# A 2-layer hybrid attention / PEER backbone on one core: weight ring from five blocks to four, u-row buffers from seven to eight

## Chip, cores and metric

One Trainium2 chip, one core. The metric is the device time of one execution in microseconds (us), lower is better.

## The reference, cut to what is computed

Two token streams of 256 tokens, width 1024 (latent `x`, context `ctx`), pass two layers. Each layer has a token mixer (attention, in layer 0 with retention) and a PEER channel mixer; each is fed by an RMS norm with gains and shifts that come from a conditioning vector. All in float32.

```python
for l in range(2):
    # six modulation vectors from silu(c) @ mod_w[l]  (1024 x 6144)
    hx = modulate(x_lat, norm1_g[l], sh1, sc1)            # ctx likewise
    yx, yc = mixer(hx, hc, w_in, w_out, ...)               # projections, attention/retention, output projection
    x_lat = x_lat + g1 * yx
    x_lat = x_lat + g2 * peer(modulate(x_lat, norm2_g[l], sh2, sc2), w_q, sub_keys, u, v)
    # the context stream does the same in layer 0 only

def peer(h, w_q, sub_keys, u, v):                          # per token: 8 heads x 16 experts = 128 rows
    q = h @ w_q                                            # 1024 x 2048
    # scores against 2 x 128 sub-keys per head, top 16 of each, top 16 of their 256 sums -> idx
    act = gelu(einsum('td,ted->te', h, u[idx]))
    return einsum('te,ted->td', softmax(top_s) * act, v[idx])
```

`u` and `v` have 16384 rows of 1024 floats (4 KB) each. Six token tiles of 128 tokens go through PEER (four in layer 0, two in layer 1), so 6 x 128 = 768 gathers of 128 rows are made from `u` and 768 from `v`.

## The kernel before

The engines' programs are written out by hand; they meet at semaphores, and each engine runs strictly in its own order.

**Weights.** All weights (blocks of `mod_w`, the input and output projections, the query projection `w_q`) stream through one ring `W` of `NW` = 5 blocks of 512 KB. The SP queue issues 240 loads in order (L497); load n waits until the block in its place, n − NW, is freed (L490, quoted below). Blocks come in groups of four, (half, part) = (0,0), (0,1), (1,0), (1,1). A group serves a piece of a product 512 columns wide: each token tile that uses it (a "unit") runs 4 matmuls of half 0 and then 4 of half 1, each of them two instructions in the profile, so 16 instructions a unit and 4 instructions a block. The first two blocks of a group are freed together when the last unit has finished half 0 (`pr_half`, `op_half`), the last two when it has finished half 1 (`pr_mm`, `op_mm`); for `mod_w` two blocks are freed after each half (`mod_mm`), for `w_q` after each pair of query heads (`pq_mm`). With five blocks, the first block of the next group is loaded while the present group is in use; the other three follow as blocks are freed.

```python
if n >= NW:
    sp.wait_ge(*blocks[n - NW][7])
```

**Gathers.** GpSimd (POOL) issues all row gathers (`u_gather`, `v_gather`, issued at L512): one gather brings 128 rows of 4 KB, 512 KB. A "slot" is one of a tile's 128 experts per token. POOL's order is two u gathers, then two v gathers which lie LAG = 36 slots behind; the first 36 slots of a window are u gathers alone. A u gather waits until the dot product `NU` = 7 slots back is done (`u_dot`, VectorE L2032), a v gather until the matmul that used its buffer is done (`v_used`, TensorE L1084). Since POOL runs in order, a u gather that waits also holds the v gathers behind it. There are two windows, tiles 0 to 3 and tiles 4 and 5. When a window's u gathers are over, its last 36 v gathers use the u buffers too.

**Beside the gathers.** The dense work of later tiles (projections, attention, retention, query scores, top-16) is cut into steps that all engines run between slots, at slots given by the table `BESIDE`. TensorE, VectorE and ScalarE take these steps in the same order as their part of the gathers.

**Before the first window** run, in this order on TensorE: four column blocks of layer 0's modulation (`ada`, L580), norm1, the projection of the context tiles (`proj(0)`, L692: 12 units in six groups of two), attention and retention of the context beside eight more blocks of `mod_w`, and the output projection (`outp(0)`, L939: four units in two groups). Meanwhile POOL loads 32 blocks of layer 1's `mod_w` into free u and v buffers (u buffers 4, 5, 6 and v buffers 5, 6) at the pace at which VectorE sums them (L1485, L1488).

**Start.** A table of biases, gains and conditioning vectors is loaded into ring block 4 (`sm`, L478 to L483) and turned by two transposes (`setup_t`); load 4 waits for them (L488). `H2` holds the normed rows of PEER and is not in use until much later.

## Time and profile before

| | us |
|---|---|
| time, 3 runs | 2670.25 median (2651.04 to 2674.83) |
| the profiled execution | 2671.68 |
| its span in the profile | 2669.9 |
| busy: TensorE (PE) | 1717.8 (64%) |
| busy: VectorE (DVE) | 1738.0 (65%) |
| busy: GpSimd (POOL), issuing gathers | 1477.8 (55%) |
| busy: ScalarE (ACT) | 377.7 (14%) |
| moved by DMA | 959.07 MB, mean 359 GB/s |

### The profile page before, as it was taken

What the parts mean: (1) busy time and instruction counts of PE and PEld (TensorE: products, weight loads), DVE (VectorE), ACT (ScalarE), POOL (GpSimd) and SP (SyncE); (2) the same over time, 40 slices, a digit from 0 to 9 for tenths busy, and PEclk for the clock granted to TensorE, in tenths of its full rate; (3) what the DMA queues carried; (4) which work ended last, traced back from release to release, by engine and by line L of the source; (5) the groups of instructions that cost most, each with busy time, mean ns of one, the idle gap of its engine ahead of it and who ended that gap; (6) DMA issues with size and microseconds to landing.
All of it is one profiled execution on the core that took longest, in us unless ns stands there. A gap on an engine that the chain in (4) does not pass through costs nothing.

```text
span 2669.9 us, 23151 instructions
## 1 busy us (share of the span) xinstructions
PE 1717.8 (64%) x7250; PEld 784.4 (29%) x7250; DVE 1738.0 (65%) x4297; ACT 377.7 (14%) x790; POOL 1477.8 (55%) x1575
## 2 busy tenths in 40 slices
PE   6899966776987764555434655677637975444335
PEld 2446652222445331222101111234432442211000
DVE  2733598776789776676645766644696776667641
ACT  1021112111122110010001211111112210101000
POOL 1100136666666766666666675771256566767774
PEclk8968987888566876666555776568867576766556
DMA  7774599999999999999999999993699899999998
GB/s 254 268 244 158 173 322 357 406 406 404 406 372 362 405 400 406 405 406 407 408 406 405 376 393 407 409 409 151 236 347 398 320 366 400 407 405 409 409 409 337
DMA packets 312521, 959.07 MB, mean 359 GB/s; under 512 B 30144, under 2 KB 65104, under 8 KB 312016
## 3 DMA queue, kind: packets, MB, share of 16 engines
q0 software_dynamic: 225792, 822.18, 78.9%
q1 hardware_dynamic: 82448, 127.47, 13.6%
q10 hardware_dynamic: 4160, 7.95, 0.8%
q8 instruction: 59, 0.97, 0.1%
q14 instruction: 62, 0.51, 0.1%
HBM read 956.43 MB, written 1.05 MB: 359 GB/s over the span
## 4 chain that ended last, share of the span: by engine, by line
DMA 37%; PE 23%; DVE 19%; POOL 11%; issue 8%; ACT 1%; SPq 0%; POOLq 0%; ACTq 0%; DVEq 0%
DMA u_rows<-in_peer_u,idx 21%; DMA v_rows<-in_peer_v,idx_turned 10%; DVE u_rows L2032 9%; POOL v_rows L512 6%; POOL u_rows L512 5%; PE ps L1084 4%; PE ps L692 4%; PE ps L732 2%; PE ps L569 2%; PE ps L750 2%; PE ps L939 2%; PE ps L580 1%; DMA wring<-in_ab_w_in 1%; DMA u_rows<-in_peer_v,idx_turned 1%; PE ps L1049 1%
## 5 line engine op out<-in xcount | busy, mean ns | idle before, releaser
L2032 DVE CUSTOM_DVE_ANT_0 u_rows<-ps,u_rows 128x1024 f32<-128x1024 f32 x768 | 926.6, 1221 | 441.2 <-DMA u_rows<-in_peer_u,idx 407.3
L512 POOL DMA_INDIRECT u_rows<-in_peer_u,idx x768 | 724.3, 943 | 668.1 <-DVE act_w L2032 370.5
L1084 PE MATMUL ps<-v_rows,spread_w 128*32 128x512 f32 x2736 | 543.1, 878 | 627.7 <-DMA v_rows<-in_peer_v,idx_turned 616.2
L512 POOL DMA_INDIRECT v_rows<-in_peer_v,idx_turned x684 | 648.6, 948 | 228.1 <-issue 188.5
L1084 PEld LDWEIGHTS ps<-v_rows,spread_w 128*32 128x32 f32 x2736 | 71.8, 127 | 931.0 <-issue 910.1
L692 PE MATMUL ps<-wring,arena 128*128 128x512 f32 x528 | 279.3, 679 | 27.2 <-DVE arena L1519 9.1
L692 PEld LDWEIGHTS ps<-wring,arena 128*128 128x128 f32 x528 | 109.0, 217 | 201.3 <-issue 155.6
L1049 PE MATMUL ps<-arena,wring 128*128 128x128 f32 (+1 forms) x768 | 159.1, 374 | 5.8 <-DMA wring<-in_peer_w_q 3.8
L1049 PEld LDWEIGHTS ps<-arena,wring 128*128 128x128 f32 x768 | 138.5, 243 | 60.7 <-issue 42.7
L569 PE MATMUL ps<-table,arena 128*128 128x128 f32 x432 | 97.3, 364 | 77.4 <-ACT arena L1137 31.0
L550 POOL DMA_DIRECT2D u_rows<-in_mod_w x20 | 14.7, 735 | 213.9 <-DVE v_rows L1488 161.0
L569 PEld LDWEIGHTS ps<-table,arena 128*128 128x128 f32 x432 | 63.0, 180 | 175.7 <-issue 74.4
L732 PE MATMUL ps<-arena 64*128 64x512 f32 (+2 forms) x128 | 101.6, 892 | 4.1 <-DVE mod_cols L1499 2.8
L939 PE MATMUL ps<-wring,arena 128*128 128x512 f32 x160 | 78.4, 640 | 9.6 <-ACT arena L1295 6.5
L750 PE MATMUL ps<-arena 128*128 128x64 f32 x416 | 83.0, 364 | 2.5 <-DVE arena L1676 2.3
L750 PEld LDWEIGHTS ps<-arena 128*128 128x128 f32 x416 | 82.8, 290 | 3.6 <-DVE arena L1676 2.7
L1392 ACT ACTIVATE act_w<-act_w 128x16 f32<-128x16 f32 x48 | 10.3, 216 | 513.1 <-DVE act_w L2032 512.9
L1362 ACT ACTIVATE arena<-ps 128x128 f32<-128x128 f32 (+1 forms) x48 | 14.8, 311 | 464.4 <-PE ps L1049 464.4
L1084 PE MATMUL ps<-resid,spread_w 128*32 128x512 f32 x192 | 41.3, 914 | 46.6 <-DMA resid<-in_peer_v,idx_turned 45.2
L580 PE MATMUL ps<-wring,silu_c 128*32 128x512 f32 x256 | 60.2, 930 | 7.9 <-DMA wring<-in_mod_w 7.8
L2032 DVE DVE_READ_ACCUMULATOR2_ANT act_w<- 128x1 f32 x768 | 63.7, 83 | 0.0
L1392 ACT ACT_TABLE_LOAD x47 | 60.3, 1283 | 0.8
(254 smaller groups left out, 1983.5 us busy)
## 6 DMA issues: line engine op xcount, KB each, us to landing
wring<-in_mod_w SPq DMA_DIRECT2D x64, 512.0 KB, 5.0
wring<-in_peer_w_q SPq DMA_DIRECT2D x64, 512.0 KB, 10.4
wring<-in_ab_w_in SPq DMA_DIRECT2D x56, 512.0 KB, 8.1
u_rows<-in_peer_u,idx POOLq DMA_INDIRECT x768, 13.6
wring<-in_swa_w_in SPq DMA_DIRECT2D x24, 512.0 KB, 10.7
v_rows<-in_peer_v,idx_turned POOLq DMA_INDIRECT x684, 13.4
u_rows<-in_mod_w POOLq DMA_DIRECT2D x20, 512.0 KB, 6.5
wring<-in_ab_w_out SPq DMA_DIRECT2D x16, 512.0 KB, 7.1
```

The lines of the kernel that those rows point to most:

```text
L512: nc.gpsimd.indirect_dma_start(out=rows, out_offset=None, in_=table, in_offset=bass.IndirectOffsetOnAxis(ap=index, axis=0)).then_inc(lande ...
L569: return nc.tensor.transpose(dst, src, ident[0:n, 0:n])
L580: mm = nc.tensor.matmul(MP(l, b)[32 * q:32 * q + 32, :], SC[:, 4 * half + q, :], w[:, q % 2, :], start=half == 0, stop=half == 1, skip_gro ...
L692: mm = nc.tensor.matmul(PS[:, unit_bank(u), :], HT[:, 4 * half + k, (t % 2) * P:(t % 2 + 1) * P], w[:, k % 2, :], start=half + k == 0, sto ...
L732: nc.tensor.matmul(PS[:, i % 2, 0:nk], q, k, start=True, stop=True).then_inc(at_s, 1)
L750: mm = nc.tensor.matmul(value_out(n, m), PT[:, m % 2, c, :], val, start=c == 0, stop=c == len(kts) - 1)
L939: mm = nc.tensor.matmul(PS[:, u % 2, :], HT[:, 4 * half + k, (t % 2) * P:(t % 2 + 1) * P], w[:, k % 2, :], start=half + k == 0, stop=half ...
L1049: mm = nc.tensor.matmul(PS[:, hp % 2, 0:nt * P], w[:, k % 4, (hp % 2) * P:(hp % 2 + 1) * P], HT[:, k, lo:lo + nt * P], start=k == 0, stop= ...
L1084: mm = nc.tensor.matmul(PS[32 * q:32 * q + 32, 6 + e, :], spread_w[:, s // PAIR % 2, 32 * c:32 * c + 32], v_buffer(v_place(x)[0])[:, e * 5 ...
L1362: nc.scalar.activation(QTB[:, hp % 2, 0:nt * P], PS[:, hp % 2, 0:nt * P], ACT.Copy).then_inc(pq_ev, 1)
L1392: nc.scalar.activation(av_[:, 1, g % 2, :], av_[:, 0, g % 2, :], ACT.Gelu).then_inc(act_done, 1)
L2032: nc.vector.tensor_tensor_reduce(UB[:, slot % NU, :], HP, UB[:, slot % NU, :], 1.0, 0.0, ALU.mult, ALU.add, av_[:, 0, g % 2, j:j + 1]).the ...
```

## The change

`NW` goes from 5 to 4 and `NU` from 7 to 8; the two arrays together keep their size (a block and a u buffer are both 4 KB per partition). The start table moves from ring block 4 to `H2[:, 1, :]`, and the wait of load 4 for the transposes goes, since load 4 now waits for block 0 to be freed. Semaphore arrays and the tables of v buffers follow from `NW` and `NU`.

```diff
-NW = 5
+NW = 4
-NU = 7
+NU = 8
...
-            sm = W[:, 4, :]
+            sm = H2[:, 1, :]
...
             for n, (_, kind, l, b, split, half, part, _) in enumerate(blocks):
-                if n == 4:
-                    sp.wait_ge(setup_t, 2)
                 if n >= NW:
                     sp.wait_ge(*blocks[n - NW][7])
...
-            turn(PS[:, 6, 0:P], W[:, 4, 0:P]).then_inc(setup_t, 1)
-            turn(PS[:, 7, 0:16], W[0:16, 4, P:2 * P], 16).then_inc(setup_t, 1)
+            turn(PS[:, 6, 0:P], H2[:, 1, 0:P]).then_inc(setup_t, 1)
+            turn(PS[:, 7, 0:16], H2[0:16, 1, P:2 * P], 16).then_inc(setup_t, 1)
```

On the SP queue the loads keep their order and what changes is what each waits for. At the start of the program, with the semaphore that each load waits for (`mod_mm`: a half of a modulation block is done; `pr_half`, `pr_mm`: a unit's first or second half is done), before:

```order
L483 DMA wring<-in_c_ctx 8x128
L497 DMA wring<-in_mod_w 128x2x512 x4
L497 DMA wring<-in_mod_w 128x2x512 [waits setup_t]
L497 DMA wring<-in_mod_w 128x2x512 [waits mod_mm] x11
L497 DMA wring<-in_ab_w_in 128x2x512 [waits mod_mm] x5
L497 DMA wring<-in_ab_w_in 128x2x512 [waits pr_half] x2
```

and with the change:

```order
L483 DMA h<-in_c_ctx 8x128
L495 DMA wring<-in_mod_w 128x2x512 x4
L495 DMA wring<-in_mod_w 128x2x512 [waits mod_mm] x12
L495 DMA wring<-in_ab_w_in 128x2x512 [waits mod_mm] x4
L495 DMA wring<-in_ab_w_in 128x2x512 [waits pr_half] x2
L495 DMA wring<-in_ab_w_in 128x2x512 [waits pr_mm] x2
```

Five projection loads stood ahead of the first wait for a unit, now four do: the first block of the second group has moved behind `pr_half`.

On POOL's queue the u and v gathers of both windows keep their order; at the end of the first window the last 36 v gathers take the buffers in another turn. There stands before:

```order
L512 DMA v_rows<-in_peer_v,idx_turned 128x1024 x2
L512 DMA u_rows<-in_peer_v,idx_turned 128x1024 x7
L512 DMA v_rows<-in_peer_v,idx_turned 128x1024 x8
L512 DMA u_rows<-in_peer_v,idx_turned 128x1024 x7
L512 DMA v_rows<-in_peer_v,idx_turned 128x1024 x8
L512 DMA u_rows<-in_peer_v,idx_turned 128x1024 x6
L512 DMA u_rows<-in_peer_u,idx 128x1024 x38
```

and with the change:

```order
L510 DMA v_rows<-in_peer_v,idx_turned 128x1024 x2
L510 DMA u_rows<-in_peer_v,idx_turned 128x1024 x8
L510 DMA v_rows<-in_peer_v,idx_turned 128x1024 x8
L510 DMA u_rows<-in_peer_v,idx_turned 128x1024 x8
L510 DMA v_rows<-in_peer_v,idx_turned 128x1024 x8
L510 DMA u_rows<-in_peer_v,idx_turned 128x1024 x4
L510 DMA u_rows<-in_peer_u,idx 128x1024 x38
```

Sixteen buffers turn there in place of fifteen; the next window starts with 38 u gathers in both.

## Rows read from the trace of the kernel before

**Rows 1.** The page: busy tenths and GB/s in 40 equal slices.

```profile
PE   6899966776987764555434655677637975444335
...
DMA  7774599999999999999999999993699899999998
GB/s 254 268 244 158 173 322 357 406 406 404 406 372 362 405 400 406 405 406 407 408 406 405 376 393 407 409 409 151 236 347 398 320 366 400 407 405 409 409 409 337
```

**Rows 2.** Windows by stage: busy of each engine, granted clock, DMA share, GB/s.

```profile
82.00:98.00 16.00, 15.33 (x49) 7.45 (x48) 14.34 (x26) 1.99 (x5) 3.90 (x6) 1.00 0.79 268
98.00:117.00 19.00, 15.94 (x46) 7.18 (x45) 14.10 (x25) 0.60 (x1) 3.75 (x6) 1.00 0.77 272
...
450.00:1800.00 1350.00, 857.50 (x3473) 346.17 (x3473) 943.00 (x2304) 198.60 (x389) 893.61 (x944) 0.68 1.02 400
```

**Rows 3.** Chain of work that ended last, projection of the context: start us, us, what.

```profile
85.48 6.19 DMA wring<-in_ab_w_in
...
91.72 1.98 PE ps L692 x4
93.70 0.44 PE ps L569 x4
94.14 0.79 PE ps L597 x8
94.92 6.99 PE ps L692 x16
...
101.93 9.11 DMA wring<-in_ab_w_in
```

**Rows 4.** Timeline of PE, 95 to 118 us.

```profile
105.68 1.98 PE L692 MATMUL ps<-wring,arena 128*128 128x512 f32 x4 [1.63 <-DMA wring<-in_ab_w_in]
108.55 1.98 PE L692 MATMUL ps<-wring,arena 128*128 128x512 f32 x4 [0.88 <-DMA wring<-in_ab_w_in]
111.09 1.98 PE L692 MATMUL ps<-wring,arena 128*128 128x512 f32 x4 [0.56 <-DMA wring<-in_ab_w_in]
```

**Rows 5.** Waits of PE, 0 to 50 us: total us, times, longest.

```profile
PE ps L580 <- DMA wring<-in_mod_w: 7.8, 5, 3.3
```

**Rows 6.** Timeline of PE, 204 to 240 us.

```profile
219.11 1.94 PE L580 MATMUL ps<-wring,silu_c 128*32 128x512 f32 x8
...
223.52 1.07 PE L580 MATMUL ps<-wring,silu_c 128*32 128x512 f32 x8
...
225.90 1.06 PE L580 MATMUL ps<-wring,silu_c 128*32 128x512 f32 x8
```

**Rows 7.** DMA issues by line, 160 to 318 us: count, KB, median us to landing.

```profile
wring<-in_mod_w SPq DMA_DIRECT2D x27, 512.0 KB, 4.7
wring<-in_ab_w_out SPq DMA_DIRECT2D x8, 512.0 KB, 4.7
```

**Rows 8.** Waits of the whole program: total us, times, longest.

```profile
POOL u_rows L512 <- DVE act_w L2032: 379.2, 282, 9.2
...
POOL v_rows L512 <- PE ps L1084: 36.0, 54, 3.3
```

**Rows 9.** Windows where the DMA engines pause beside gathers, columns as in rows 2.

```profile
318.00:400.00 82.00, 60.85 (x271) 50.40 (x269) 69.18 (x214) 12.53 (x36) 34.57 (x37) 0.87 0.92 320
400.00:440.00 40.00, 18.54 (x67) 7.78 (x68) 32.16 (x89) 9.03 (x16) 25.45 (x27) 0.63 0.92 325
...
780.00:850.00 70.00, 63.90 (x288) 40.42 (x288) 67.39 (x132) 21.45 (x35) 43.27 (x46) 0.65 0.92 336
...
1520.00:1550.00 30.00, 14.79 (x62) 4.45 (x61) 24.19 (x58) 8.88 (x13) 16.20 (x17) 0.73 0.83 307
...
1920.00:2000.00 80.00, 31.72 (x166) 26.06 (x165) 77.38 (x225) 9.84 (x25) 39.03 (x42) 0.68 0.92 327
...
2080.00:2160.00 80.00, 75.33 (x278) 40.15 (x278) 60.21 (x152) 20.40 (x50) 44.71 (x48) 0.56 0.88 311
```

**Rows 10.** DMA issues by line, 450 to 650 us, columns as in rows 7.

```profile
wring<-in_ab_w_in SPq DMA_DIRECT2D x19, 512.0 KB, 11.0
...
u_rows<-in_peer_u,idx POOLq DMA_INDIRECT x68, 18.2
```

**Rows 11.** Timeline of PE in the second window, 2008 to 2220 us.

```profile
2010.67 6.70 PE L692 MATMUL ps<-wring,arena 128*128 128x512 f32 x8 [1.72 <-DVE g_row L1452]
...
2018.29 3.70 PE L692 MATMUL ps<-wring,arena 128*128 128x512 f32 x8
...
2033.12 3.11 PE L692 MATMUL ps<-wring,arena 128*128 128x512 f32 x4 [1.89 <-DMA wring<-in_swa_w_in]
...
2215.21 2.08 PE L1049 MATMUL ps<-arena,wring 128*128 128x128 f32 x8 [3.79 <-DMA wring<-in_peer_w_q]
```

## The prediction

> **What bounds the kernel now.** I read the page's 40 slices first [rows 1]. They show three regimes. From the seventh slice (400 us) to the 27th (1800 us), and from about 2000 us on, the DMA engines are busy nine tenths or more and move 400 to 409 GB/s: the gathers. In the first five slices TensorE is busy eight or nine tenths and DMA moves 158 to 268 GB/s: the dense work before the first gather, fed by the weight ring. Around slice 28 (1800 to 1900 us) there are no gathers at all. The windows by stage say the same with numbers: from 450 to 1800 us the DMA share is 1.02 with TensorE at 857 of 1350 us, while from 82 to 117 us TensorE works 31 of 35 us at full clock and DMA is at 0.77 to 0.79 [rows 2]. So a larger u buffer can gain only where DMA pauses beside gathers, and a smaller ring can lose mainly where there are no gathers: there TensorE's delay is the program's delay, and it moves everything behind it.
>
> **Ring from five to four, projection of the context.** The chain of waits shows this stage alternating between L692 and a load of `ab_w_in` [rows 3]. A load is issued at 85.48, when a unit's second half ends; it lands 6.19 us later, at 91.67; the four instructions that use this block start at 91.72; then come two short pieces and a whole unit (6.99 us for 16 instructions, so 1.75 us for a block's four), and the next load of the chain is issued at 101.93. With five blocks the first of a group is already there, so the load at 85.48 is the group's fourth block, the third of the four issued after the last unit's first half. With four blocks it becomes the group's third, and the fourth is issued directly behind it. It must be used after the third, so each change of group costs at least its 1.75 us where the loads come close together, and the distance between landings where they come slower. TensorE waits before each of three blocks in a row at 105.68, 108.55 and 111.09, so landings there are (111.09 - 105.68) / 2 = 2.7 us apart [rows 4]. Six groups have five changes: 4 x 1.75 + 2.7 = 9.7 us. Lower bound 0, if something else on the way is later (the rows name nothing); upper bound five times the widest distance, 108.55 - 105.68 = 2.87, so 14.4.
>
> **Modulation at the start.** TensorE waits 7.8 us in five pieces for `mod_w` here [rows 5]. The fifth load, which started as soon as the small table was turned, must now wait for block 0, and from then on two pairs of loads take turns. I count the pair's second block (1.3 us at 400 GB/s for 512 KB) once behind the longer wait and about 1.2 us over the following three groups: 2.5 us. Bounds: 0, if the engines' rate sets this stage anyway, and 7.8, if the waits double. The wait on the transposes that goes is worth nothing, since a later one takes its place.
>
> **Modulation beside attention, output projection.** With four blocks, the pair for a half is issued when the half before the previous one ends. Near the end of this stage one half runs 219.11 to 221.05 and the half after next starts at 225.90 [rows 6], which leaves 4.85 us; loads land in a median of 4.7 us here [rows 7], and the pair's second a little later: 0.5 us. Where halves are farther apart it costs nothing. In the output projection the first block of the second group used to be there; now it is issued half a unit (3.5 us) ahead of its use and takes 4.7 [rows 7]: 1 us. Bounds for both together 0 to 3. Before the gathers the ring costs 9.7 + 2.5 + 0.5 + 1.0 = 13.7 us, between 0 and 25.
>
> **The ring beside gathers.** Here loads land later (11.0 us [rows 10]) and TensorE already waits for the last block of a group, 1.89 us before 2033.12 and 3.79 us before 2215.21 [rows 11]. These waits will grow by some 2 to 6 us at perhaps four places. Queued behind them on TensorE are matmuls of v rows, which hold v buffers, and VectorE steps that hold dot products. But the DMA engines stay at 1.02 [rows 2] with up to fifteen gathers issued ahead, 15 x 1.3 = 19 us of work, so nearly all of it is covered: 2 us, between 0 and 10.
>
> What the row says of a deeper gather queue: a weight block issued into it lands after 11.0 us, a u gather after 18.2 [rows 10], so blocks pass the gathers that wait. The Trainium skill (DMA: Bandwidth & Descriptors, "Queues, rings and completion order") has the rule for it: each DMA engine takes turns between the queues that have work, a packet at a time. By that rule the eighth gather adds nothing to a block's time; if instead blocks stood in one line with the gathers, each would land one gather (1.3 us) later and the 2 us above would be about 5. The trace agrees with the rule.
>
> **u buffers from seven to eight.** POOL waits 379.2 us in 282 pieces for a dot product before a u gather, and only 36.0 us for v buffers [rows 8]. Most of this costs nothing, as DMA is full meanwhile. What can be won is the time in which DMA pauses, 1.03 less the share, times the length [rows 9]: 82 x 0.11 = 9.0; 40 x 0.11 = 4.4; 70 x 0.11 = 7.7; 30 x 0.20 = 6.0; 80 x 0.11 = 8.8; 80 x 0.15 = 12.0; 47.9 us in all. One more buffer lets POOL run one slot farther ahead before it stops: a u gather and the v gather behind it, 2 x 1.3 = 2.6 us of DMA work for each stall, or 1.3 us where only u gathers are issued. It does not make VectorE or TensorE faster, so a stretch in which one of them is always busy gains once, not at every pause. VectorE works 69 of 82, 67 of 70 and 77 of 80 us in the first, third and fifth window, TensorE 75 of 80 in the last [rows 9]. So I take each window as one stall: 1.3 for the first and the fifth, which begin with u gathers alone, 2.6 for the other four: 13.0 us. Bounds: 0, and all 47.9. I stay near the low end, because four of six windows are bound by an engine.
>
> **Moved v gathers.** In a window's last 36 v gathers one more buffer turns. DMA runs at 409 GB/s there [rows 1], so nothing is won or lost.
>
> **Sum.** 13.7 + 2.0 - 13.0 = +2.7 us. On the profiled execution's 2671.7 us that is 2674.4. This execution lies 1.4 us above the median of the three runs, 2670.25, so I forecast 2673. About 1% is what a measurement of this kernel can tell from no change: its three runs span 0.9%.
>
> **Rivals.**
>
> *Pauses are short and separate (faster).* POOL's waits for dots average 379.2 / 282 = 1.3 us [rows 8], less than the 2.6 us of an added slot. If the DMA pauses in the six windows are made of such pieces with recoveries between, four fifths of 47.9 go: -38 + 13.7 + 2 = -22, and 2648 us. Against it: VectorE or TensorE hardly rest in four of the windows. Chance 0.14.
>
> *Depth buys nothing.* If every pause is the engine's own pace, and the extra gather is repaid in the next stretch, only the losses stay: +15.7, 2686 us. For it speaks the same busy time; against it, the window from 1520 to 1550 with one long wait (9.2 us at most [rows 8]). Chance 0.16.
>
> *TensorE's clock falls in the early stage (slower by over 1%).* The clock is granted at full there with waits up to 1.63 us between blocks [rows 2, 4]. With four blocks each group waits longer, at its first block too. If that brings the lower level, 1.2 GHz, matmuls take about twice as long: eight instructions of L692 took 6.70 us in one place and 3.70 in the next [rows 11]. A group has 32 instructions of 0.44 us: 14 us more for each group that runs slowly. With one group the time is 2687, with two 2701; it decides from the second group on. The Trainium skill (TensorE: Matmul & The Clock Gate, "Part 1: The HAM clock gate") says that the throttled clock is the default and activity releases it, which speaks for this rival; the full clock in rows 2 in spite of waits speaks against it so far. Chance 0.12.
>
> The forecast, losses and gains about equal, has 0.58. Its own range is 2660 to 2687. The range of 8 in 10 takes in the first two rivals and one slow group: 2648 to 2700. Faster by over 1% (under 2643.5) needs most of the first rival: 0.11. Slower by over 1% (over 2697) comes from the clock, or from losses at their upper bounds with no gain: 0.13. Within 1%: 0.76.
>
> **What would show it.** In the trace of the changed kernel the first u gather should be issued about 14 us later than before. TensorE should wait for `ab_w_in` between 50 and 150 us some 10 us more in total, now before a group's first and fourth block too, at an unchanged clock. The six windows of rows 9, shifted by the same 14 us, should together lose about 35 us instead of 48. Elsewhere the DMA share should stay at 1.02 to 1.03. The prediction is wrong in its first part if the first gather is not late, in its second if the pauses shrink by over 25 us or not at all, and in its cover if DMA shows new pauses at changes of weight group beside gathers.

## The result, and the profile after

| | before | with the change |
|---|---|---|
| time, median of 20 runs (us) | 2655.16 (2642.04 to 2674.83) | 2675.78 (2664.42 to 2699.03) |
| ratio, runs set against each other | | 1.0062, 95% [1.0039, 1.0085] |
| the profiled execution (us) | 2671.68 | 2682.0 |
| its span (us) | 2669.9 | 2680.2 |

The change makes the kernel 0.62% slower, 16.5 us at 2655: little, but the interval leaves out 1. The medians of the table are 20.6 us apart; the ratio, made from runs set against each other, is the figure used below, and its interval, 10.4 to 22.6 us, holds both. All ratios leave out executions more than 1.5% above the fastest of their kernel, which touches e3 (four of twelve) and e12 (two of twelve) below most. The forecast of 2673 us lies 3 us from the new median, and that closeness flatters it. The profiled execution before, from which the sum was made, was near the slow end of the 20 runs, which spread over 33 us: it lies 16.5 us above their median. The working gave +2.7 us, and +16.5 were measured. So what has to be explained is a difference of 14 us in a sum that "came out right".

The page of the changed kernel, its busy tenths and its rates, and the DMA issues, answering to [rows 1]:

```profile
PE   6899975766887765555444655677647974445335
...
DMA  6766499999999999999999999993799899999998
GB/s 226 253 230 204 135 332 348 405 406 405 405 387 347 406 400 406 406 404 408 408 406 406 401 372 407 409 409 146 244 359 405 317 358 366 407 404 409 409 409 349
```

The three regimes stand as before. In the first two slices DMA moves less than in [rows 1] (226 and 253 GB/s for 254 and 268): with a block less in flight the weights come more slowly. From slice 8 most slices read 400 to 409 again.

Waits of PE in the changed kernel, 0 to 50 us and 50 to 165 us (total us, times, longest); before they were [rows 5] and, for `ab_w_in`, 7.5 us in 8 pieces:

```profile
PE ps L578 <- DMA wring<-in_mod_w: 12.0, 6, 4.6
...
PE ps L690 <- DMA wring<-in_ab_w_in: 14.8, 11, 4.2
```

The timeline of PE in the projection of the context (the idle time ahead of each piece in brackets), answering to [rows 4]:

```profile
101.92 7.11 PE L690 MATMUL ps<-wring,arena 128*128 128x512 f32 x16
108.87 0.60 PE L567 MATMUL ps<-table,arena 128*128 128x128 f32 x4
111.81 5.37 PE L690 MATMUL ps<-wring,arena 128*128 128x512 f32 x8 [2.34 <-DMA wring<-in_ab_w_in]
118.89 1.98 PE L690 MATMUL ps<-wring,arena 128*128 128x512 f32 x4 [1.71 <-DMA wring<-in_ab_w_in]
121.29 1.13 PE L690 MATMUL ps<-wring,arena 128*128 128x512 f32 x2 [0.42 <-DMA wring<-in_ab_w_in]
```

A unit of 16 instructions runs without a pause, and then comes the wait that did not exist before, ahead of the first block of the next group (2.34), and further ones ahead of its third and fourth. That is the edit read directly. The eight instructions at 111.81 also took 5.37 us where eight took 3.70 at 97.13: the granted clock was 0.72 from 112 to 118 us.

Two single instructions give milestones. The end of the projection is the end of its last matmul, the start of the gathers is the first u gather on POOL. In the changed kernel, from the timelines of PE and of POOL:

```profile
164.80 1.88 PE L690 MATMUL ps<-wring,arena 128*128 128x512 f32 x4
...
325.56 1.01 POOL L510 DMA_INDIRECT u_rows<-in_peer_u,idx  x1 [47.09 <-DVE idx L1956]
```

and in the kernel before:

```profile
151.31 1.88 PE L692 MATMUL ps<-wring,arena 128*128 128x512 f32 x4
...
317.75 1.01 POOL L512 DMA_INDIRECT u_rows<-in_peer_u,idx  x1 [46.17 <-DVE idx L1958]
```

The projection ends 13.5 us later, but the first gather is only 7.8 us later. Between them lies attention beside eight blocks of modulation, and there TensorE's granted clock differed. Windows of before and of after, 164 to 237 us, columns as in [rows 2]. Before:

```profile
164.00:237.00 73.00, 72.43 (x313) 39.85 (x314) 20.88 (x65) 13.91 (x37) 0.00 (x0) 0.61 0.65 220
```

After:

```profile
164.00:237.00 73.00, 69.94 (x333) 35.08 (x331) 23.09 (x69) 15.09 (x42) 1.45 (x2) 0.77 0.79 261
```

TensorE is busy nearly all the time in both, and its clock reads 0.61 before and 0.77 after. More instructions are done in less busy time. Whether this belongs to the change is a question for repeats (below: it does not).

Beside the gathers, three views. First the waits of POOL over the whole program, answering to [rows 8]:

```profile
POOL u_rows L510 <- DVE act_w L2030: 272.1, 242, 10.3
...
POOL v_rows L510 <- PE ps L1082: 161.3, 133, 7.0
```

The wait for a dot product has gone from 379.2 to 272.1 us, as the edit promises, and the wait for a v buffer from 36.0 to 161.3. The queue stops in another place, not less. Second, the six windows of [rows 9], moved by the delay of their gathers:

```profile
326.00:408.00 82.00, 60.13 (x270) 50.12 (x269) 69.37 (x216) 12.75 (x36) 35.92 (x39) 0.88 0.93 328
408.00:448.00 40.00, 18.79 (x69) 7.96 (x70) 32.60 (x90) 9.02 (x16) 24.85 (x26) 0.65 0.87 312
...
788.00:858.00 70.00, 58.20 (x287) 36.83 (x285) 67.35 (x134) 21.45 (x35) 41.02 (x43) 0.71 0.90 335
1528.00:1558.00 30.00, 14.01 (x62) 4.36 (x60) 25.05 (x62) 8.88 (x13) 18.00 (x20) 0.73 0.94 351
1927.00:2007.00 80.00, 32.87 (x173) 26.39 (x172) 77.39 (x225) 9.83 (x25) 40.60 (x44) 0.68 0.94 341
2087.00:2167.00 80.00, 75.39 (x279) 40.30 (x278) 59.85 (x151) 20.41 (x50) 43.75 (x48) 0.56 0.87 304
```

By the prediction's own measure, 1.03 less the share, they lose 8.2 + 6.4 + 9.1 + 2.7 + 7.2 + 12.8 = 46.4 us; before they lost 47.9. Only the fourth window is plainly better (0.83 to 0.94, 3.3 us), and the 100 us after it are worse, 1.01 at 395 GB/s, where before they had 1.03 at 406.

Third, a place where a pause is new: the last group of `w_q` blocks. Timeline of PE in the changed kernel, with [rows 11] at 2215.21 as its counterpart:

```profile
2218.98 1.06 PE L1082 MATMUL ps<-v_rows,spread_w 128*32 128x512 f32 x8
2224.21 1.39 PE L1047 MATMUL ps<-arena,wring 128*128 128x128 f32 x8 [4.17 <-DMA wring<-in_peer_w_q]
2230.23 2.08 PE L1047 MATMUL ps<-arena,wring 128*128 128x128 f32 x8 [4.63 <-DMA wring<-in_peer_w_q]
```

the instruction of VectorE and the gather of POOL that are released behind it:

```profile
2232.77 0.30 DVE L1869 MAX8 top_vals<-ps 128x8 f32<-128x128 f32 x1 [9.88 <-PE ps L1035]
...
2236.49 0.94 POOL L510 DMA_INDIRECT u_rows<-in_peer_u,idx  x1 [9.92 <-DVE act_w L2030]
```

and the window around it:

```profile
2222.00:2242.00 20.00, 9.54 (x58) 4.65 (x58) 9.91 (x28) 1.56 (x2) 7.09 (x8) 0.74 0.83 301
```

Before, one wait of 3.79 us stood here, POOL's longest wait was 5.74 us, and DMA did not pause:

```profile
2212.00:2232.00 20.00, 9.34 (x46) 3.62 (x50) 15.02 (x41) 1.56 (x2) 11.05 (x12) 0.65 1.04 394
```

The order of events fits one chain: TensorE waits twice for weights, so VectorE's top-16 has no scores, so its next dot product is late, so POOL does not issue, and after some ten us the queue of gathers runs dry: 20 x (1.04 - 0.83) = 4.2 us of DMA lost.

### The profile page after: what moved, and what is told of

Same layout as the page of the kernel before. It is cut to its first block, busy times and chain, and to the rows that moved or that the text cites. A ratio compares the mean times of both kernels' runs of the same rounds, so it can differ in the third digit from the quotient of the medians.

```text
span 2680.2 us, 23151 instructions
## 1 busy us (share of the span) xinstructions
PE 1691.3 (63%) x7250; PEld 777.4 (29%) x7250; DVE 1734.3 (65%) x4297; ACT 377.9 (14%) x790; POOL 1476.1 (55%) x1575
## 4 chain that ended last, share of the span: by engine, by line
DMA 40%; PE 24%; DVE 17%; POOL 9%; issue 7%; ACT 1%; SPq 0%; ACTq 0%; POOLq 0%; DVEq 0%
DMA v_rows<-in_peer_v,idx_turned 20%; DMA u_rows<-in_peer_u,idx 13%; DVE u_rows L2030 7%; POOL v_rows L510 5%; PE ps L1082 5%; PE ps L690 5%; POOL u_rows L510 4%; PE ps L937 2%; DMA wring<-in_ab_w_in 2%; PE ps L1047 2%; PE ps L730 2%; PE ps L567 2%; DMA u_rows<-in_peer_v,idx_turned 2%; PE ps L578 1%; PE ps L748 1%
## 5 line engine op out<-in xcount | busy, mean ns | idle before, releaser
L2030 DVE CUSTOM_DVE_ANT_0 u_rows<-ps,u_rows 128x1024 f32<-128x1024 f32 x768 | 926.9, 1221 | 441.2 <-DMA u_rows<-in_peer_u,idx 406.1
L1082 PE MATMUL ps<-v_rows,spread_w 128*32 128x512 f32 x2736 | 526.5, 858 | 630.3 <-DMA v_rows<-in_peer_v,idx_turned 620.0
L690 PE MATMUL ps<-wring,arena 128*128 128x512 f32 x528 | 273.2, 666 | 38.2 <-DMA wring<-in_ab_w_in 16.5
L1047 PE MATMUL ps<-arena,wring 128*128 128x128 f32 (+1 forms) x768 | 168.9, 390 | 10.9 <-DMA wring<-in_peer_w_q 8.8
L1047 PEld LDWEIGHTS ps<-arena,wring 128*128 128x128 f32 x768 | 146.0, 254 | 67.0 <-issue 47.0
L730 PE MATMUL ps<-arena 64*128 64x512 f32 (+2 forms) x128 | 94.4, 831 | 4.1 <-DVE mod_cols L1497 2.8
L937 PE MATMUL ps<-wring,arena 128*128 128x512 f32 x160 | 77.7, 631 | 16.1 <-ACT arena L1293 6.5
L1360 ACT ACTIVATE arena<-ps 128x128 f32<-128x128 f32 (+1 forms) x48 | 14.8, 311 | 468.2 <-PE ps L1047 468.2
L578 PE MATMUL ps<-wring,silu_c 128*32 128x512 f32 x256 | 61.3, 823 | 12.3 <-DMA wring<-in_mod_w 12.3
L1869 DVE MAX8 top_vals<-ps 128x8 f32<-128x128 f32 x80 | 22.1, 293 | 68.6 <-PE ps L1035 66.7
L2030 DVE DVE_READ_ACCUMULATOR2_ANT act_w<- 128x1 f32 x768 | 63.7, 83 | 0.0
## 6 DMA issues: line engine op xcount, KB each, us to landing
wring<-in_peer_w_q SPq DMA_DIRECT2D x64, 512.0 KB, 10.5
```

The costliest lines, as they stand in the source:

```text
L578: mm = nc.tensor.matmul(MP(l, b)[32 * q:32 * q + 32, :], SC[:, 4 * half + q, :], w[:, q % 2, :], start=half == 0, stop=half == 1, skip_gro ...
L690: mm = nc.tensor.matmul(PS[:, unit_bank(u), :], HT[:, 4 * half + k, (t % 2) * P:(t % 2 + 1) * P], w[:, k % 2, :], start=half + k == 0, sto ...
L730: nc.tensor.matmul(PS[:, i % 2, 0:nk], q, k, start=True, stop=True).then_inc(at_s, 1)
L937: mm = nc.tensor.matmul(PS[:, u % 2, :], HT[:, 4 * half + k, (t % 2) * P:(t % 2 + 1) * P], w[:, k % 2, :], start=half + k == 0, stop=half ...
L1047: mm = nc.tensor.matmul(PS[:, hp % 2, 0:nt * P], w[:, k % 4, (hp % 2) * P:(hp % 2 + 1) * P], HT[:, k, lo:lo + nt * P], start=k == 0, stop= ...
L1082: mm = nc.tensor.matmul(PS[32 * q:32 * q + 32, 6 + e, :], spread_w[:, s // PAIR % 2, 32 * c:32 * c + 32], v_buffer(v_place(x)[0])[:, e * 5 ...
```

## Experiments

All time is cut at five instructions, the starts of the first u gather and of the dot products (L2032, after the change L2030) number 1, 512, 513 and 768, and at the projection's two ends (the end of its first instruction and of its last). "Window 1" is from the first to the 512th dot product, "window 2" from the 513th to the 768th. The kernels of a job share runs of the kernel before; the first column of times is those shared runs' median.

| kernel | job, before | ratio, 95% | projection from, to | clock 164 to 237 | first u gather | window 1 | window 2 |
|---|---|---|---|---|---|---|---|
| before, profiled first | 2655.2 | | 50.7, 153.2 | 0.61 | 317.8 | 1444.6 | 702.0 |
| with the change | 2655.2 | 1.0062 [1.0039, 1.0085] | 54.3, 166.7 | 0.77 | 325.6 | 1444.2 | 706.3 |
| e1 before | A 2783.75 | 1.0022 [0.9983, 1.0061] | 50.9, 151.5 | 0.75 | 308.3 | 1507.9 | 746.9 |
| e2 ring 4, u 7 | A | 1.0088 [1.0058, 1.0119] | 52.2, 162.9 | 0.56 | 329.2 | 1500.7 | 754.6 |
| e3 the change | A | 0.9998 [0.9956, 1.0041] | 51.5, 162.3 | 0.93 | 309.3 | 1488.1 | 750.1 |
| e4 change + 1 early place | A | 0.9957 [0.992, 0.9995] | 50.4, 153.1 | 0.62 | 316.3 | 1478.1 | 757.6 |
| e5 ring 4, u 7 | B 2812.72 | 1.0056 [1.0022, 1.0089] | 51.4, 162.5 | 0.63 | 328.2 | 1521.7 | 761.9 |
| e6 ring 5, u 6 | B | 1.0061 [1.0024, 1.0099] | 50.9, 151.7 | 0.55 | 322.7 | 1535.5 | 762.2 |
| e7 ring 5, u 7, 9 early places | B | 0.9913 [0.9875, 0.9951] | 48.1, 140.1 | 0.83 | 295.7 | 1501.0 | 757.1 |
| e8 ring 4, u 8, 9 early places | B | 0.9886 [0.9832, 0.9941] | 48.2, 139.2 | 0.97 | 284.1 | 1505.8 | 763.1 |
| e9 ring 4, u 7, v 9 | C 2662.51 | 1.0088 [1.0048, 1.0128] | 53.5, 167.7 | 0.55 | 339.7 | 1443.9 | 709.5 |
| e10 ring 4, u 7 | C | 1.0080 [1.0042, 1.0117] | 52.8, 164.4 | 0.88 | 315.9 | 1443.7 | 710.0 |
| e11 change + 1 early place | C | 1.0021 [0.9988, 1.0054] | 50.8, 152.8 | 0.75 | 307.4 | 1444.7 | 703.0 |
| e12 ring 4, u 8, 9 early places | C | 0.9949 [0.9912, 0.9987] | 48.5, 139.0 | 0.61 | 309.9 | 1445.8 | 705.8 |

Jobs A, B and C ran on three different chips. In A and B the same kernel takes 2784 and 2813 us, 5 to 6% more than in the first comparison and in job C. The expectations put this down to the chip; but each chip was measured in one job only, so it can't be told apart from whatever else differed then. The difference turned out to be useful: it separates the two halves of the change. e8 has six timed executions, e9 seven, the other kernels of the jobs twelve.

**Job A: is it the ring, is it the depth?**

e1 is the kernel before, unchanged, as a measure of what a ratio of equal kernels looks like.

> The kernel before, a second time, as a yardstick: a ratio of 1.000 within its interval, and a second profile of the same program. Theory A (the two profiles of before and after differ partly by TensorE's granted clock between 150 and 240 us, which is not a part of the change): the first u gather is issued up to 8 us earlier or at the same time as in the first profile (317.8 us), and the clock between 164 and 237 us differs from 0.61. Rival B (the clock there follows from the program): clock and first gather as in the first profile, within 1 us.

It measured 1.0022 [0.9983, 1.0061]. With the clock at 0.75 where the first trace of the same program had 0.61, its first gather came at 308.3 instead of 317.8: the same program, so the rival, that the clock follows from the program, is out.

e2 undoes one half of the change:

```diff
 NW = 4
-NU = 8
+NU = 7
```

> Ring of four alone, seven u buffers as before. Theory A (the early stage pays for the ring, the eighth u buffer bought next to nothing): 14 to 18 us slower than before, ratio about 1.006, the same as the changed kernel within 3 us; context projection done 13 to 14 us late as in the changed kernel. Rival B (the eighth buffer returns the 13 us that I forecast and the ring costs more than forecast, beside the gathers too): 27 to 30 us slower than before, ratio about 1.011.

It measured 1.0088, between the two forecasts (1.006 and 1.011): the ring of four costs 25 us by itself on this chip.

e3 is the changed kernel again.

> The changed kernel beside the others on the same chip: ratio 1.004 to 1.009 as measured. Theory A: within 3 us of the run with four blocks and seven u buffers. Rival B: 10 us or more faster than that run.

It measured 0.9998 [0.9956, 1.0041], below the range expected, and the rival's case came true. Here the change is no loss that the interval shows. Against e2, run beside it, the eighth buffer gives 0.9%, 25 us; by the plain means of all twelve executions each (1.0019 and 1.0087 of before's) it is 0.7%, 19 us. In the two traces window 1 is 12.6 us shorter and window 2 4.5 us; the 19.9 us between their first gathers go with the clock (0.93 and 0.56).

e4 keeps the change, but until the gathers begin the eighth u buffer serves as a fifth place of the ring. Loads below a limit may take extra places; POOL waits for the last use of such a place before its first gather.

```diff
+        EXTRA = [(UB[:, 7, :], 84)]
+        w_in = [sem(f"w_in{i}") for i in range(NW + len(EXTRA))]
...
+        for n in range(len(blocks)):
+            freed, k = free_w.pop(0)
+            while k >= NW and n >= EXTRA[k - NW][1]:
+                freed, k = free_w.pop(0)
...
+            for k in range(NW, NW + len(EXTRA)):
+                if EXTRA[k - NW][1] == 84:
+                    pool.wait_ge(*W_LAST[k])
```

> The changed kernel, but u buffer 7, which is idle until the gathers, serves as fifth place of the ring for the first 84 loads (up to the output projection). Theory A (the loss is made before the first gather): the whole 14 to 16 us come back, ratio to before 0.998 to 1.001; PE waits for mod_w and ab_w_in before 165 us are 15 us in total as before, not 27. Rival B (the ring of four also costs beside the gathers, out(3) and the last query projection above all): only 8 to 10 us come back and the ratio stays at 1.002 to 1.004.

It measured 0.9957, below the range expected. The projection ends at 153.1 like before's, so the early loss is the ring's fifth place and nothing else of the change. Against e3 the place gives 0.4%, 11 us, near the 11 us between before's and the ring of four's projections in this job (151.5, and 162.9 and 162.3).

**Job B: each size against its neighbours.**

e5 repeats e2.

> Ring of four and seven u buffers once more, since the chip of the last four runs was about 5% slower than the one of the changed kernel's first timing, and the changed kernel's ratio differed between them (1.006 there, 1.000 here). Theory A (the ring costs the same on any chip, 0.6 to 0.9%; the eighth buffer is worth nothing where DMA runs at 405 GB/s without pause and about 0.9% where it pauses): ratio to before 1.006 to 1.009 in either case. Rival B (the ring's cost itself depends on the chip): ratio under 1.003 or over 1.012.

1.0056, just under the range expected: the loss repeats, a little smaller.

e6 goes the other way in depth, with the ring as it was (one early `mod_w` block moves from u buffer 6 to v buffer 7):

```diff
-NU = 7
+NU = 6
...
-        EARLY_W = [UB[:, 4, :], UB[:, 5, :], UB[:, 6, :], VB[:, 5, :], VB[:, 6, :]]
+        EARLY_W = [UB[:, 4, :], UB[:, 5, :], VB[:, 7, :], VB[:, 5, :], VB[:, 6, :]]
```

> Depth alone in the other direction: five ring blocks and six u buffers (the early blocks that used u buffer 6 go to v buffer 7). No change before the first gather. Theory A on a chip where DMA is full: within 6 us of before, ratio 1.000 to 1.003; on a chip where DMA pauses: 20 to 40 us slower. Rival B (a slot of depth is worth 13 us anywhere, as forecast): 13 to 20 us slower, ratio 1.005 to 1.0075.

1.0061: on this chip a u buffer less costs 17 us. That is under the 20 to 40 us of theory A and inside the range of the rival, "13 us anywhere"; taken alone e6 speaks for the rival, and only job C, where depth gave nothing, is against its "anywhere". Its window 1 is the longest of all, 1535.5, in a profiled execution that was itself 0.8% above its median.

e7 has before's sizes, the start table in `H2`, and four extra ring places before the gathers:

```diff
 NW = 5
 NU = 7
...
+        EXTRA = [(VB[:, 7, :], 84), (VB[:, 2, :], 40), (VB[:, 3, :], 40), (VB[:, 4, :], 40)]
```

> Five blocks and seven u buffers as before, but before the gathers the ring has nine places: idle v buffers 2, 3, 4 for the first 40 loads and v buffer 7 for the first 84. Theory A (before the gathers TensorE's waits for weights are on the path; there are 15 us of them until 165 us in the kernel before): 10 to 15 us faster than before, ratio 0.994 to 0.996; PE waits for mod_w and ab_w_in under 5 us. Rival B (something else, the clock or VectorE, takes the time back): within 5 us of before.

e8 has the change's sizes and the same idea (four places of its own and five lent, nine in all; its expectation counts them as ten):

```diff
 NW = 4
 NU = 8
...
+        EXTRA = [(UB[:, 7, :], 84), (VB[:, 7, :], 84), (VB[:, 2, :], 40), (VB[:, 3, :], 40), (VB[:, 4, :], 40)]
```

> The changed kernel's four blocks and eight u buffers, with ten places before the gathers (u buffer 7 as well). It separates the ring's cost before the gathers from that beside them. Theory A on a chip where DMA is full: like the run with nine places and seven u buffers, plus 3 to 5 us for the waits beside gathers that the changed kernel's trace shows from 2150 us on. On a chip where DMA pauses: 15 to 25 us faster than that run. Rival B: the loss beside the gathers is 10 us or more on a chip where DMA is full.

They measured 0.9913 and 0.9886, for e7 more than the 0.994 to 0.996 expected, and for e8 8 us less than e7, not 15 to 25. Both end the projection at 140 us, some 12 us ahead of before's, and no wait for `ab_w_in` is left. That accounts for half of e7's 24 us; the other half was not traced. The list of PE's waits for weights in e7, 0 to 175 us:

```profile
PE ps L598 <- DMA wring<-in_mod_w: 3.5, 3, 2.9
...
PE ps L598 <- DMA v_rows<-in_mod_w: 2.4, 1, 2.4
```

**Job C: where DMA is full, what is the limit?**

In this job the kernel before is as fast as in the first comparison. e9 gives the freed block to the v buffers, since in the changed kernel POOL waited for these:

```diff
 NW = 4
-NU = 8
-NV = 8
+NU = 7
+NV = 9
```

> The changed kernel with its freed block given to the v buffers: ring of four, seven u buffers, nine v buffers (ten in the second window become eleven). Theory 1 (in the windows the v buffers, not the u buffers, are what the gathers wait for once there are eight u buffers, and where DMA is full neither gives anything): window 1, from the first dot product to the last of its 512, within 3 us of that of the ring of four with seven and eight buffers; the ratio to before as that of the ring of four with seven u buffers, within 0.002. Rival (v buffers are the limit): window 1 shorter than with seven u and eight v buffers by 5 us or more, and the ratio smaller by 0.003 or more. On a chip with pauses in its DMA (before above 2750 us) a v buffer may give what a u buffer gave, 10 to 20 us.

Window 1 is 1443.9, within 0.3 us of the others, and the ratio 1.0088: the first theory holds, and a v buffer is worth nothing at seven u buffers. (Nine v buffers beside eight u buffers need one more block of memory and were not tried.)

> The ring of four alone, seven u buffers, once more beside the others. Theory 1 (the ring costs about 15 us ahead of the gathers on any chip): ratio 1.005 to 1.009, end of the context projection 10 to 14 us later than before's 152.6. If this chip is as fast as the first (before below 2700 us), theory 1 expects the same ratio as the whole change had there, 1.006, since the eighth u buffer bought nothing where DMA is full. Rival (the eighth buffer bought some 10 us on the first chip too, and the ring cost 25): ratio 1.009 or more.

e10, the ring of four alone, measured 1.0080 [1.0042, 1.0117]. The whole change had 1.0062 against the same kernel in another job. So the eighth u buffer is worth 0.2% here across two jobs, and the intervals do not even show that. The traces are sharper: window 1 is 1443.7 with seven and 1444.2 with eight. Only window 2 differs, 710.0 and 706.3.

The waits of POOL in e10 from 850 to 1500 us:

```profile
POOL u_rows L510 <- DVE act_w L2030: 89.0, 77, 5.0
...
POOL v_rows L510 <- PE ps L1082: 9.6, 23, 2.2
```

and in the changed kernel in the same stretch:

```profile
POOL v_rows L510 <- PE ps L1082: 72.0, 57, 5.2
...
POOL u_rows L510 <- DVE act_w L2030: 37.9, 55, 2.3
```

About a hundred us of waiting in both, at 405 and 402 GB/s, for one buffer or for the other. This is what waiting at a full resource looks like: remove one reason and the next one takes all of it.

> The changed kernel whose eighth u buffer serves as the fifth place of the ring for the first 84 loads, before the gathers. Theory 1: the loss in the context projection is gone (no later than 154 us at its end), ratio 0.995 to 1.001: on a chip as fast as the first it is nearly that of before (0.999 to 1.001), since only the early ring had cost something; on a slower chip 0.995. Rival (the loss is beside the gathers): ratio still 1.004 or more on a fast chip.

e11 measured 1.0021 [0.9988, 1.0054], a little above the range expected: the early loss is gone (152.8), and the middle value would fit a small loss beside the gathers, though the interval holds 1. Its PE waits 2.39 and 5.06 us for the last group of `w_q`, like the changed kernel.

> Ring of four, eight u buffers, and nine ring places in all before the gathers (one u buffer and four v buffers lent to the ring for its first 84 and 40 loads). Theory 1 (the waits for weights ahead of the gathers go, here in full, and the gathers start 12 us or more earlier): ratio 0.987 to 0.994 on any chip, end of the context projection near 139 us. Rival (the earlier weights only take DMA time from the early mod_w loads, so that the first gather is not earlier on a fast chip): ratio 0.998 or more there.

e12 measured 0.9949 [0.9912, 0.9987], just outside the range expected, and clear of the rival's 0.998 only in its middle value: the projection ends at 139.0, 14 us ahead of before's. By the plain means of all executions it is 0.9973, and the medians are 2658.6 beside 2662.5, so in this job the gain is small and its size uncertain; the rival is not ruled out. The changed kernel itself was not run in this job. In job B the same design, e8, has 2777.8 beside 2812.7. The trace of e12 shows the clock at 0.61 in the stretch behind the projection, and its first gather, at 309.9, is only 8 us ahead of the first trace's.

## Why the prediction was right and where it failed

**What bounds the kernel: right, with two loose readings of [rows 1].** The first slice has TensorE at six tenths, not eight or nine. Within the stretches given for the gathers some slices move less than 400 GB/s: 357 in the first of them, 362 and 372 near 750 to 850 us, 376 and 393 near 1500, 320 and 366 after 2070. No term hangs on either.

**The projection of the context: right in its length.** The term was 9.7 us. The projection takes 102.5, 100.6 and 100.8 us in three traces with a ring of five and 112.4, 110.7, 110.8, 111.1, 114.2 and 111.6 in six with four: means 101.3 and 111.8, so 10.5. The places are those that were named too: new waits stand ahead of a group's first block, and of its third and fourth. The prediction put all of it down to waits, some 10 us more. Between the two first traces the projection grew by 9.9 us and the waits for `ab_w_in` by 7.3 (7.5 to 14.8); part of the rest is work at the lower clock, 1.7 us in the one place shown above.

**The start: right.** 2.5 us were forecast for the modulation; the projection starts on average at 50.8 with five and at 52.6 with four, 1.8 us later. With the 10.5 that makes 12.3 at the projection's end, 152.1 to 164.4.

**Beside attention and the output projection: 1.5 us forecast, not separable.** The stretch from the projection's end to the first gather varies from 144.9 to 172.0 us, mostly with the clock. Fitting over all 14 traces a straight line in the clock and a step each for the ring of four and for the nine early places leaves 2 us for the ring, with single traces up to 4 us off. It agrees with the term, and does not show it.

**"The first u gather about 14 us later": wrong in one trace, for a reason outside the change.** It came 7.8 us later. Two traces of one program, e1 and before, differ by 9.5 us at this point, and e2 and e3, with the same ring, by 19.9. Such a milestone is not a good test of an edit when a stretch with a wandering clock lies ahead of it; the projection's end, which lies before that stretch, is.

**The ring beside the gathers: mechanism right, too small.** The term was 2 us, between 0 and 10, at places where TensorE already waited. The two waits named, for `swa_w_in` and `w_q` in the second window, grew from 3.3 and 3.8 us in total to 5.5 and 8.8 (in e10 to 5.4 and 8.2), and the wait for `w_out`, which was not named, from 1.4 to 3.6 (4.3): 9.4 us in all. I held that nineteen us of queued gathers would cover nearly all. But two waits that follow each other closely, 4.17 and 4.63, add up behind VectorE and POOL to 9.9, and the queue ran dry for 4.2 us. Window 2 takes 702.0 us in before's trace, and 710.0 and 709.5 with a ring of four and seven u buffers: some 8 us is the ring's price here, inside the bounds and four times the term. Job A has the same step (746.9 in e1, 754.6 in e2), though there two kernels that are alike from the first gather on, e3 and e4, also differ by 7.5. The eighth buffer gives some 5 of it back (706.3, 703.0 and 705.8). The sign named for a wrong cover, a new pause of DMA at a change of weight group, is there.

**The rule for the queues: it held.** A weight block issued in the full stretch (458 to 658 us) lands after 11.1 us, before 11.0 [rows 10]; a u gather after 21.2, before 18.2. From the DMA issues of the changed kernel:

```profile
wring<-in_ab_w_in SPq DMA_DIRECT2D x20, 512.0 KB, 11.1
...
u_rows<-in_peer_u,idx POOLq DMA_INDIRECT x69, 21.2
```

The deeper queue delays only itself, the u gathers by 3.0 us and the v gathers by 2.0 (18.4 to 20.4), which is about the u and v gather that one slot adds (2.6). The Trainium skill (DMA: Bandwidth & Descriptors, "Queues, rings and completion order") says that each DMA engine takes turns between the queues with work, and the trace agrees. What the same row also shows, I had not asked: where DMA is full, one more gather in flight lands later by about the time for which it was issued earlier.

**The depth of the u buffers: wrong, and this is the step that failed (the term of -13.0 us).** I wrote that one more buffer "lets POOL run one slot farther ahead before it stops" and took from this 13.0 us at six windows, one added slot for each. The six windows lost 46.4 us instead of 47.9, where 35 were forecast, and window 1 lasted 1444.6, 1444.2, 1443.7, 1443.9, 1444.7 and 1445.8 us with seven or eight u buffers, eight or nine v buffers, four or five blocks. The lead is there (POOL waits 272.1 us for dot products instead of 379.2, and a u gather lands 3 us later), but it bought no time: in the window from 1520 us the share rose from 0.83 to 0.94 and the next 100 us gave two thirds of it back, and the last 127 slots of window 1 took 345.8 us before and 346.0 after. The first part of the working said itself that four of six windows are bound by an engine; consistent with that would have been 0 for those four, and about 5 us for the others. Even that would have been wrong in its place: the two others (400 and 1520 us) lie in window 1, which gained nothing, and the 5 us came in window 2. Nearest is the rival "depth buys nothing", at +15.7 us, beside +16.5 measured. I gave it 0.16, and it should have been the forecast. That its sum fits so closely is luck in part: the ring cost some 8 us beside the gathers where it had 2, and the buffer gave some 5 back where it had 0. The ring alone was measured at 1.0080, 21 us (e10).

**Why the time was hit all the same.** A gain of 13 us, of which some 5 exist, was taken from a base 15 us above the median of the 20 runs (2670.25 beside 2655.16). That the two errors cancel is luck. The range, 2648 to 2700, holds the median; within 1% was the right case, but the forecast's reason, losses and gains about equal, held only in job A.

**In job A the balance is the one forecast.** There e3 measures 0.9998 and e2 1.0088. Windows 1 and 2 together take 2254.8 and 2255.3 us in its two traces with seven u buffers (e1, e2), and 2238.2 and 2235.7 with eight (e3, e4): 18 us. In job B the traces do not separate the two: 2283.6 and 2258.1 with seven (e5, e7), 2268.9 with eight (e8). There only the ratios speak, 17 us between six and seven buffers (e6), and 8 us between e7 and e8 although e8 has the smaller ring beside the gathers. From the windows by stage, 450 to 1800 us, of e1 (the kernel before on that chip):

```profile
450.00:1800.00 1350.00, 803.00 (x3280) 325.57 (x3278) 903.84 (x2225) 184.62 (x352) 851.73 (x898) 0.70 0.99 382
```

The share is 0.99 where the first trace had 1.02 [rows 2]: DMA pauses inside this stretch, and depth has something to fill. One such place, in e1's POOL timeline:

```profile
1088.98 0.94 POOL L512 DMA_INDIRECT u_rows<-in_peer_u,idx  x1 [0.30 <-issue]
1097.19 0.94 POOL L512 DMA_INDIRECT u_rows<-in_peer_u,idx  x1 [7.27 <-DVE act_w L2032]
```

POOL stops for 7.27 us, and between 1090 and 1100 us DMA is at 0.57. Why DMA pauses there and not in the first trace is open. A hint lies in the packets: of those of 4 KB between 450 and 1800 us the slowest in a hundred take over 173 ns in each of the six traces of the first comparison and job C, and over 294 to 399 ns in the eight of jobs A and B, while the median is 164 and 161 ns. No single late gather was followed to its packet.

**The rival that the clock falls: not as priced, but the clock did dip.** In the projection it read 0.92 and 1.00 before (50 to 100 and 100 to 150 us), and with the change 0.89 and 0.97 (50 to 100 and 100 to 160 us). No whole group ran at the lower level. Windows of before and of after, 104 to 124 us:

```profile
104.00:124.00 20.00, 16.93 (x45) 7.40 (x44) 11.53 (x20) 0.00 (x0) 2.89 (x4) 1.00 0.78 282
...
104.00:124.00 20.00, 15.53 (x41) 6.81 (x39) 10.53 (x18) 0.60 (x1) 2.89 (x4) 0.91 0.73 249
```

In this stretch the clock is 0.91 in e2, e5 and e10 and 0.82 in e9, all with a ring of four, and 1.00 in e3, which has one too, and in all eight traces with five or nine places. The dip did not add its full length: e3 without it has a projection of 110.8 us, e2 and e5 with it 110.7 and 111.1; e9, with the lowest clock, has the longest, 114.2.

The budget where the kernel before takes about 2660 us, each term from the traces: 12.3 before the gathers, about 2 by the fit, 4.3 in window 2, together 18.6 beside 16.5 measured (95%: 10.4 to 22.6).

## What to carry to other kernels

Depth in front of a resource that is already full bought only longer queueing here; before pricing a buffer, take the stretches where the resource pauses, strike those in which an engine is always busy, and ask of the rest whether what is issued earlier is not simply missing afterwards. Where memory is to be shared between two rings whose needs lie in different stages, lend it instead of cutting it: the u and v buffers as weight places until the gathers begin gave 0.9% and 1.1% in job B and 0.5% in job C (0.3% by the mean of all executions), more than either way to split it. And a sum from one profiled execution should be carried to the median as a difference: add it to the median of many runs, not to the execution's own time.

## What the runs showed of the hardware that was not expected

**The clock ahead of the gathers wanders from run to run.** In the stretch of attention and modulation behind the projection, TensorE's granted clock was between 0.55 and 0.97 from 164 to 237 us in 14 traces, also for one and the same program (before: 0.61 and 0.75; the changed kernel: 0.77 and 0.93; ring 4 with u 7: 0.56, 0.63 and 0.88). The time from the projection's end to the first gather follows it: 172.0 us at 0.55 (e9), 144.9 at 0.97 (e8), and about 59 us for each 1.0 of clock, with a correlation of -0.97. Windows of e9 and of e3, 164 to 237 us, the first for TensorE alone (us, busy and count, then clock, share, GB/s):

```profile
164.00:237.00 73.00, 70.23 (x265) 0.55 0.66 222
```

and the second:

```profile
164.00:237.00 73.00, 69.88 (x372) 35.35 (x374) 24.54 (x75) 15.69 (x42) 1.44 (x2) 0.93 0.76 259
```

TensorE is busy 70 of 73 us in both, with 265 and 372 instructions done. A swing of up to 27 us there is larger than the whole change and may explain much of the spread of the runs: among the 20 executions with the change the time falls with the mean clock of the span (2699.0 us at 0.705, 2664.9 at 0.732, correlation -0.89). In which stretch the clock differed in these 20 is not on record. What decides the level in a given run, no trace here tells.

**Jobs on different chips differ in more than a factor.** The projection, set by TensorE and the weight loads, takes the same time in both kinds (100.6 us in e1, 102.5 in the first trace); the gathers do not (window 1 is 1507.9 us and 1444.6). So the same edit is worth different amounts: the eighth buffer gave some 5 us in the traces of one kind, too little for the ratios to show, and 17 to 25 us in job A. Whether the chip itself makes the difference, no run here tells.
